# Where the causal-mask products stand in the attention score steps of a two-block network

## The reference, cut to what matters

```python
# differential attention: 8 heads, two maps of 64 each, block of 128 queries
s = jnp.einsum('bhmqd,bhmkd->bhmqk', qb, kb).astype(jnp.float32) * scale
mask = jnp.arange(lo, hi)[:, None] >= jnp.arange(hi)[None, :]
p = jax.nn.softmax(jnp.where(mask, s, -jnp.inf), axis=-1)
a = (p[:, :, 0] - lam * p[:, :, 1]).astype(v.dtype)
outs.append(jnp.einsum('bhqk,bhkd->bhqd', a, vb))
...
# latent attention, once in each of two layers: 8 heads, one map of 64 + 32
sc = jnp.where(mask, sc, -jnp.inf)
p = jax.nn.softmax(sc, axis=-1).astype(v.dtype)
return jnp.einsum('bhqk,bkhe->bqhe', p, v)
```

## Time and profile before

| | |
|---|---|
| Median of 3 runs | 4291.12 us (4286.86 to 4293.38) |
| Profiled execution: its own time, and its span | 4289.11 us, 4287.3 us |
| PE busy, instructions | 3567.9 us (83%), 17556 |
| PEld busy | 2705.7 us (63%) |
| DVE busy | 2420.2 us (56%) |
| ACT busy | 1809.7 us (42%) |
| Mean granted TensorE clock | 0.910 of full speed (2.4 GHz) |

### The profile page before, as it was taken

How to read it: one execution, slowest core, us unless ns; L and a number is a source line. 1 busy time by engine, 2 the same in 40 slices (tenths; PEclk the granted TensorE clock), 3 DMA queues, 4 the chain that set the end, 5 groups by cost and what they waited for, 6 DMA issues and landing times. The chain is left out here.

```text
span 4287.3 us, 52640 instructions
## 1 busy us (share of the span) xinstructions
PE 3567.9 (83%) x17556; PEld 2705.7 (63%) x17556; DVE 2420.2 (56%) x3882; ACT 1809.7 (42%) x2971; POOL 284.6 (7%) x358
## 2 busy tenths in 40 slices
PE   5998979599999177859999936998968889989687
PEld 4775658488888144647888725776744467867343
DVE  2224666799889536469998865512335454023455
ACT  2114652388888110118888832313433232144332
POOL 0000001000000200000000020000011100000111
PEclk9998999699999589869999967999979989999798
DMA  5212225399999563629999964322123244121321
GB/s 187 100 64 75 60 80 182 134 399 398 398 398 381 197 238 139 213 79 390 399 398 399 398 236 169 149 73 58 46 104 100 76 158 154 56 61 37 134 83 57
DMA packets 403706, 799.18 MB, mean 186 GB/s; under 512 B 98502, under 2 KB 149222, under 8 KB 399336
## 3 DMA queue, kind: packets, MB, share of 16 engines
q1 hardware_dynamic: 380524, 713.40, 46.0%
q0 software_dynamic: 13824, 50.34, 3.3%
q10 hardware_dynamic: 9216, 33.56, 1.9%
HBM read 661.25 MB, written 135.95 MB: 186 GB/s over the span
## 5 line engine op out<-in xcount | busy, mean ns | idle before, releaser
L314 DVE TENSOR_TENSOR experts_down_lo<-weights_down,experts_down_hi 128x1024 fp32r<-128x1024 f32 x256 | 301.9, 1221 | 54.3 <-ACT experts_down_hi L310 51.5
L314 DVE TENSOR_TENSOR experts_gate_lo<-weights_gate,experts_gate_hi 128x1024 fp32r<-128x1024 f32 x256 | 299.2, 1221 | 58.9 <-ACT experts_gate_hi L310 57.8
L363 PE MATMUL project_acc<-project_wh,project_hh 128*128 128x512 f32 (+2 forms) x768 | 292.6, 381 | 24.7 <-DVE project_wl L314 24.7
L310 ACT CAST experts_gate_hi<-weights_gate 128x1024 fp32r<-128x1024 f32 x256 | 255.1, 1056 | 115.4 <-PEq L128 68.1
L314 DVE TENSOR_TENSOR experts_up_lo<-weights_up,experts_up_hi 128x1024 fp32r<-128x1024 f32 x256 | 296.1, 1217 | 1.3 <-ACT experts_up_hi L310 0.5
L364 PE MATMUL project_acc<-project_wl,project_hh 128*128 128x512 f32 (+2 forms) x768 | 287.7, 375 | 0.0
L365 PE MATMUL project_acc<-project_wh,project_hl 128*128 128x512 f32 (+2 forms) x768 | 287.5, 374 | 0.0
L310 ACT CAST experts_down_hi<-weights_down 128x1024 fp32r<-128x1024 f32 x256 | 257.2, 1052 | 30.0 <-DMA weights_down<-in_moe_w_down_dram 29.7
L2521 PE MATMUL mixout_acc<-mixout_w,mixout_mT 128*128 128x512 f32 x512 | 255.2, 651 | 13.7 <-ACT mixout_mT L2603 10.5
L310 ACT CAST experts_up_hi<-weights_up 128x1024 fp32r<-128x1024 f32 x256 | 255.1, 1057 | 11.1 <-DMA weights_up<-in_moe_w_up_dram 8.7
L2222 ACT COPY project_row<-project_acc 128x512 f32<-128x512 f32 (+2 forms) x96 | 51.8, 539 | 419.6 <-PE project_acc L365 415.9
(11 more groups left out here) (425 smaller groups left out, 7855.0 us busy)
## 6 DMA issues: line engine op xcount, KB each, us to landing
weights_gate<-in_moe_w_gate_dram SPq DMA_DIRECT2D x256, 512.0 KB, 13.3
weights_up<-in_moe_w_up_dram SPq DMA_DIRECT2D x256, 512.0 KB, 12.3
weights_down<-in_moe_w_down_dram SPq DMA_DIRECT2D x256, 512.0 KB, 11.8
scratch_y<-experts_y ACTq DMA_DIRECT2D x64, 512.0 KB, 6.3
pool_ada<-in_ada_w_dram SPq DMA_DIRECT2D x16, 1536.0 KB, 6.9
mixout_row<-scratch_proj SPq DMA_DIRECT2D x16, 1368.0 KB, 5.9
project_raw<-in_w_in_dram SPq DMA_DIRECT2D x8, 2048.0 KB, 9.8
scratch_proj<-project_row SPq DMA_DIRECT2D x64, 256.0 KB, 2.0
```

Source lines behind the costliest of these rows:

```text
L310: return act.copy(hi, src)
L314: return dve.tensor_tensor(lo, src, hi.bitcast(F32), ALU.subtract)
L363: nc.tensor.matmul(acc, a[0][k], b[0][k], start=(start and k == 0), stop=False)
```

## The change

In `scores`, the loop over the two parts is split. The first loop does the waits and the score products of the wide and then of the narrow part. A second loop over the parts does the mask products, each part's last one raising `s_ready` as before. So no mask product stands between the wide and the narrow scores any more, and both parts' `s_ready` come behind all score products of the step. The number of products is the same. In the differential phase four mask products follow each other, in the latent phases two.

```diff
@@ scores(n), lines 691 to 704
                     for part, i in enumerate(tiles_of(n)):
                         if before >= 0:
                             pe.wait_ge(exp_done, EXPS * before + maps * (part + 1))
                         cols = (i + 1) * P
                         for c in range(0, cols, HALF):
...
+                    for part, i in enumerate(tiles_of(n)):
+                        cols = (i + 1) * P
                         for mp in range(maps):
                             last = nc.tensor.matmul(scores_of(n, part, mp)[:, cols - P:cols], identr[:, :], maskr[:, :],
                                                     start=False, stop=True)
                         last.then_inc(s_ready, 1)
```

## The result

The changed kernel takes 4297.85 us (median of 18 runs, 4290.84 to 4303.21), the kernel before 4291.11 (18 runs, 4285.75 to 4296.72). The ratio is 1.0016 with a 95% interval of 1.0009 to 1.0023: slower by 6.7 us, 3.9 to 9.9 by the interval. I had forecast 12.4 us more. The time lies inside the stated range (4296 to 4312), near its low end, and just under the forecast's own (4298 to 4309). The loss is smaller than the 8.6 us that I had called too small to tell from none; with 18 runs of each kernel the interval still shuts out zero.

What follows compares the result with a forecast made beforehand. The prediction took TensorE's work as the limit, with VectorE's output copy becoming its last wait in latent A, C and D. Latent +17.0 and differential -4.6 gave +12.4 us on the 4291.1 median: 4303.5 us, range 4296 to 4312.

Steps and rivals of the forecast that it cites:

- D: Step of each head with the latent phases' narrow scores at 0.86 us: latent +0.46 us, differential +0.22 us.
- B: Step of each head with the latent phases' narrow scores at 0.43 us: latent +0.04 us, differential -0.36 us.
- C: Step of each head with the latent phases' narrow scores at 0.64 us: latent +0.35 us, differential -0.36 us.
- A: Step of each head with the latent phases' narrow scores at 0.21 us: latent +0.21 us, differential -0.08 us.
- The sum of the latent steps: Latent phases, 64 steps: 1.06 us for each head, x 16 heads = +17.0 us, bounds 14 and 20.
- the differential term: Differential phase, 32 steps: -0.58 us for each head, x 8 = -4.6 us, bounds 0 and -11.5.
- Masks in a row: Two more masks at the differential step's end, 0.11 us each, +0.22; two adjacent masks in latent B, +0.04.
- The first (nothing given back): Rival: latent phases lose 20 us and the differential phase gives nothing back, 4311 us; chance 14%.
- The second: Rival: latent delay mostly absorbed, line 755 late only in A, 3.4 - 4.6 = -1.2 us, 4290 us; chance 12%.
- The third (the drain is all there is): Rival: tiling-mode drain alone counts, 0.36 us saved in each of 32 differential steps, -11.5, 4279.6 us; chance 6%.

Runs made afterwards that it cites:

- the differential phase alone: Against the kernel before, masks moved behind both parts' scores only in the differential phase, latent phases in the old order: 4285.83 us, ratio 0.9990.

## Why the prediction was right, point by point

**What the change costs and where.** Right: the loss in the latent phases, a smaller gain in the differential one, D there slower and B and C faster. The first reduction starts at the same distance behind the first score product in all four kinds of step, 2.20 or 2.21 us (in A 3004.92 - 3002.72). It moved by the narrow scores' length, as worked out.

**The sum of the latent steps** was too large: 1.06 us a head for 0.60, 17.0 us for 9.6. This is the term that was mis-sized, by 7.4 us; the differential term was off by 0.8 the other way. So the mechanism was right and the size was not: the loss is about half of what I forecast, and the time lies near the low end of the range. There are two main reasons.

First, the gap between the second reduction and the output copy. I took the 0.06 us in step A as VectorE's own and carried it into C and D. It was a wait: the copy needs the narrow output products too, and they had just ended. Timeline of the kernel before, step A:

```profile
3006.40 0.78 PE L720 MATMUL mla_o_ps<-mla_v,mla_aT 128*128 128x64 f32 x6
```

Their end, 3007.18, is 0.11 before the copy of 3007.29, the same distance as in D before the change, where the row names that wait (0.21 <-PE). The earlier trace rows had a sign of it: the second reduction starts 0.07 before the end of the first one's row (3006.95 against 3005.80 + 1.22 = 3007.02), so a gap behind a row was not VectorE's own. With nothing left to wait for, the changed kernel's copy starts 0.08 us before the row of the reduction ends (3006.26 against 3006.06 + 0.28 = 3006.34). In C and D it is 0.09 before. That is 0.14 or 0.15 us in each of A, C and D. In D it is all of the difference: +0.31 for +0.46.

Second, C had room that I didn't look for. Timeline of the kernel before, step C: the copy of the second transposes and the load of the turn that needs it.

```profile
3021.04 0.48 ACT L780 COPY mla_aT<-mla_tp 128x384 f32<-128x384 f32 x1
...
3021.57 0.39 PEld L673 LDWEIGHTS mla_tp<-constants,mla_q 128*96 128x96 f32 x4
```

Eight output loads at 0.11 us from 3020.59 are through at 3021.47, and the turn could only start after 3021.52 + 0.05. So 0.10 us of the later output was absorbed there, which with the 0.14 above makes +0.12 of +0.35 (to 0.01). I had checked this wait in D alone, where there is no such room (27.78 right behind the loads), and had said "Nothing there gives the delay back" of all.

**Step A, another way than I said.** I put its 0.21 us on the output load and wrote that this covered ScalarE's lateness. It is the other way round: the output load is only 0.06 later (3.87 us after the step's start, 3.81 before), and the wide exponential waits for the first bias (3005.80 -> 3004.92 against starts of 3003.82 and 3002.72, 0.22 later). The copy behind it ends at 3007.53 and the turn starts at 3007.59. The experiment with the output copy moved shows it: A's output load is back in place and A is not shorter. So the size was nearly right (+0.15 for +0.21) and its place wrong: it is luck that ScalarE's path, which I hadn't priced, costs nearly what I had put on the output load.

**The differential phase**: -0.48 for -0.58 a head. A, B and D are within 0.02. C, which I took as B, is -0.29: its narrow exponentials end closer to the wide scores' end. The first narrow load went out at 503.80, released by them after 0.19 idle, and a load takes 0.11, so it isn't hidden as in B. By an estimate from the pace of 0.107 for each tile and pass and one load of 0.11, the wide scores end 1.61 us behind their start in B, at 494.56 + 1.61 = 496.17, 0.15 after that load went out (496.02), and 1.39 behind their start in C, at 503.84, only 0.04 after it.

**Masks in a row**: 0.22 or 0.23 us for two more, as said, by the rows of all four steps (0.46 or 0.47 from the first mask load to the transposes, where a pair took 0.24). The two adjacent masks in the latent phases cost B 0.02, where I had 0.04.

**Rivals.** The first (nothing given back) fell with the differential phase alone. The second (latent delay mostly absorbed, +3.4 us there for the forecast's +17.0) was wrong in saying that only A is late, since C and D pay too; but the measured +9.6 lies near the middle of the two, and the total of 5.8 to 6.7 us about midway between its -1.2 and my +12.4. The third (the drain is all there is) fell twice: A and D of the differential phase are gated by the narrow exponentials, and the latent loss outweighs the gain. The rule in the Trainium skill, "TensorEngine Tiling (Array Packing)", section Tiling Modes, that changing the tiling mode drains TensorE, agrees with this case: without the wide masks B is 0.57 us shorter, and only 0.23 of that are products. Rival 3 left out who waits for the products that are moved.

## What to carry to other kernels

When a product that releases another engine is moved behind more work, first add up what that engine has queued behind the release, and then look at who waits for the last of it. Read every gap in that queue for what ended it, since a gap that is a wait goes when its owner becomes late, and look in every kind of step for the wait that has room. Moving the masks out from between the scores paid 0.34 us in the step where nothing gated the scores behind them (B) and cost 0.22 in the one where a wait stood there anyway (D): masks in such a wait are free.

## What the runs showed of the hardware that was not expected

- VectorE's rows overlap when the next instruction waits for nothing: the copy starts 0.08 or 0.09 us before the end of the reduction's row in A, C and D of the changed kernel. A chain of its instructions is shorter than the sum of its rows.
- A weight load that had waited for a semaphore went out while the products before it still ran: in B of the changed kernel the load starts at 496.02, released by ScalarE, 0.15 us before the wide scores are through by the estimate above, and is hidden; in C it starts 0.04 before that, and by the same estimate some 0.06 or 0.07 us of its 0.11 show.
- A pair of 128-row products between products of 64 rows costs 0.57 us in step B of the differential phase, two more of them in a row 0.22 or 0.23.
